# Hyena filter spectrum by folded lags: tap pairs summed and differenced over n and 512 - n, two lag tiles per frequency tile

## The chip, the cores and the metric

The kernel runs on one core of a Trainium2 chip. The metric is the device time of one execution in microseconds (us). Engines: PE (TensorE, matmuls), DVE (VectorE), ACT (ScalarE), POOL (GpSimd), SP (SyncE, which issues most of the DMAs).

## The reference

Two transformer-like blocks run one after the other on x of shape (1, 512, 1024) in float32. The first mixes a Hyena branch (512 channels) and a bidirectional mLSTM branch, then has cross attention to a memory of 256 tokens and a feed-forward layer; the second has a gated convolution, a linear recurrent unit and a gated feed-forward layer. What the change touches is the spectrum of the Hyena filters:

```python
def _hyena_filter_spectrum(L, w1, b1, fr1, w2, b2, fr2, w3):
    ...
    hid = jnp.sin(fr2.astype(f32) * (hid @ w2.astype(f32) + b2.astype(f32)))
    filt = (hid @ w3.astype(f32)).reshape(L, HYENA_ORDER, FILTER_DIRS, D_HYENA)
    ...
    filt = filt * jnp.exp(-t * jnp.abs(deltas))[:, None, None, :]
    fwd = filt[:, :, 0]
    bwd = jnp.flip(filt[1:, :, 1], axis=0)
    two_sided = jnp.concatenate([fwd, jnp.zeros((1, HYENA_ORDER, D_HYENA), f32), bwd], axis=0)
    return jnp.fft.rfft(two_sided, axis=0)
```

L is 512. The real part of the spectrum at frequency k is a cosine sum over the lags n = 0 to 511 of (forward tap + backward tap), the imaginary part a sine sum of their difference, with angle 2 pi n k / 1024; frequency 512 has the alternating sum alone.

## The kernel before

All weights come through one ring of four 128x1024 **strips**: SP loads strip n into slot n % 4 once PE has finished strip n - 4 (semaphore `pe_done`, lines 455 to 465). ACT casts the strip to its fp32r high part (`high`, line 1003), POOL writes the low part (`low`, line 479), and PE makes every product out of three fp32r matmuls: high x high, high x low, low x high (`three`, lines 518 to 520). Each engine works down a queue in program order; ACT's calls `ahead(n)` cast strip n + 3. All order is written by hand with semaphores, and nothing is scheduled by a planner.

**Start, v/o strips and units.** PE goes through eight v/o strips (`vo_strip`, lines 585 to 587), four on banks 0 to 3 and four on banks 4 to 7 of the accumulator. Among their matmuls stand eight **units** (`unit(q)`, line 564), one for each order (2) and tile of 128 lags (4). A unit is two fp32 matmuls on `hid` and `hneg` (the hidden layer with the sign of the backward half turned), which give the sum and the difference of the forward and backward taps of these 128 lags; for the tile that holds lag 0 the skip gain is added by one matmul with a single row (line 568). Unit 2 waits for ACT to have copied v out of banks 0 to 3 (`vo_kept`, tile `VX`, line 1105). DVE multiplies a unit by the decay (`sum_and_difference`, line 1492, tile `sd`), ACT casts it into the high half of its tap pair (`unit_high`, line 1063), DVE writes the low half (`unit_low`, line 1499, semaphore `f_pair`). Tap pairs are the tiles `taps`, 128 lags x (512 sum + 512 difference).

**Spectrum.** When all eight pairs are there, PE goes through five steps s, one strip each (`for s in range(N_SPEC)`). Step s, for s from 0 to 3, gives 128 frequencies: for part 0 (cosine, on the sums) and part 1 (sine, on the differences) and both orders it contracts over four lag tiles, 4 x 3 matmuls a bank, four banks. Step 4 is frequency 512 alone, two banks. Even steps use banks 0 to 3, odd ones banks 4 to 7. In the middle of step 0 stand two fp32 matmuls with `ones` (lines 627 and 628): the column sums of squares of the memory (`mem_sq`, reduced by DVE at line 1528) and of x. ACT empties the banks (`spectrum(s)`, line 1131) into `Hc`, `Hs` and `HB` and signals `spec_out`; between these stand the norm's Sqrt, the casts of the memory (`NH`) and the strips' casts.

**After it** come the gate strip, eight q/k strips with their convolution on DVE, the z strips beside the mLSTM, and the rest of both blocks.

Of the kernel before, what the change touches and what calls it, by code (L numbers as in the profile page):

```python
# [35 lines left out]
P = 128  # L36
T = 512
# [10 lines left out]
N_VO, N_SPEC, N_GATE, N_QK, N_Z, N_HY = 8, 5, 1, 8, 12, 4  # L48
# [37 lines left out]
UNITS = 2 * (T // P)  # L86
STEPS = 4 * 2 * TT
# [71 lines left out]
def build(nc, A, out):  # L159
    ctx = ExitStack()  # L160
    with ctx:
# [24 lines left out]
        sd = [at(f"sd{i}", 2 * T, (164 + 4 * i) * KB + 128) for i in range(2)]  # L186
# [75 lines left out]
        acc = at("acc", T, small + 13856)  # L262
        misc = at("misc", 80, small + 15904)
# [67 lines left out]
        f_pair = sem("f_pair")  # L331
        norm_sum = sem("norm_sum")
# [181 lines left out]
        def _(pe):  # L514
# [97 lines left out]
            for s in range(N_SPEC):  # L612
                n = S_SPEC + s
                pe.wait_ge(lo_ready, (n + 1) * 2)
# [14 lines left out]
                mm.then_inc(pe_done, 1)  # L629

            strip(S_GATE, S_GATE % RING, 2, XH, XL)
            for u in range(N_QK):
                strip(S_QK + u, (S_QK + u) % RING, (u + 3) % 4, XH, XL,
                      taken=E_GATE + u - 2 if u >= 3 else None, needs=(spec_out, N_SPEC) if u in (1, 2) else None)
# [363 lines left out]
        def _(act):  # L998
# [86 lines left out]
            act.activation(hneg[:], hid[:], ACT.Copy, scale=col("sgn")).then_inc(f_neg, 1)  # L1085
# [30 lines left out]
            ahead(7)  # L1116
            act.wait_ge(pe_done, S_VO + 8)
# [308 lines left out]
        def _(dve):  # L1426
# [58 lines left out]
            def sum_and_difference(q):  # L1485

                dve.wait_ge(f_tap, q + 1)
                if q >= 2:
                    dve.wait_ge(f_pair, q - 1)
                b = (4, 6, 0, 2, 0, 2, 0, 2)[q]  # L1490
                dec = tile(decay, q % TT).rearrange("p (a c) -> p a c", a=1).to_broadcast([P, 2, T])
                dve.tensor_tensor(sd[q % 2][:].rearrange("p (a c) -> p a c", a=2), ps[:, b:b + 2, :], dec, ALU.mult
                                  ).then_inc(f_sd, 1)
                dve.wait_ge(f_sd, q + 1)

            def unit_low(q):
# [637 lines left out]
def _tables():  # L2134
    n = np.arange(T)[:, None]
    k = np.concatenate([np.arange(0, T, 2), np.arange(1, T, 2)])[None, :]
    ang = 2 * np.pi * ((n * k) % (2 * T)) / (2 * T)
    cos, sin = np.cos(ang), np.sin(ang)
    cos_nyq = cos.copy()
    cos_nyq[:, 0] = np.where(np.arange(T) % 2 == 0, 1.0, -1.0)  # L2140
# [13 lines left out]
    spec = [[blk(cos, k_, s) for k_ in range(TT)] + [blk(sin, k_, s) for k_ in range(TT)] for s in range(TT)]  # L2154
    spec.append([blk(cos_nyq, k_, 0) for k_ in range(TT)] + [zero] * TT)
# [13 lines left out]
    return spec, order, feat, decay  # L2169
# [112 lines left out]
```

## Time and profile before

| | |
|---|---|
| median of 3 runs | 1810.19 us (1808.28 to 1810.41) |
| the profiled execution's own time | 1808.34 us |
| its span, first to last instruction | 1806.5 us |
| mean granted clock of PE | 0.983 of full |
| PE busy | 1735.1 us, 96% of the span |
| ACT, DVE, POOL busy | 667.0, 877.3, 831.5 us |
| spectrum stage | 83.2 us to 139 us of the span |

The profile is one execution. Times in the rows are microseconds from the start of the span; "busy" is the time in which an engine had an instruction running, and a window's row gives the busy time and the number of instructions of each engine in turn. A timeline's row begins with start and length in us, "x2" stands for two such instructions in a row, and the bracket at its end tells how long the engine was idle before and whose result ended that. The matmuls overlap: one of 128x512 lasts 0.39 us in a row and the next starts 0.23 us after it.

### The profile page before, as it was taken

Reading aid. Unit: us, or ns where it says so; the run is one execution under the profiler, and the core shown is the slowest. Engines: PE = TensorE matmul, PEld = TensorE weight load, DVE = VectorE, ACT = ScalarE, POOL = GpSimd, SP = SyncE. Lnnn points to the kernel's source line nnn. Section 1 sums busy time; section 2 is a strip of 40 time slices with the busy share of each in tenths; the row PEclk is TensorE's granted clock in tenths of the full one; section 3 lists DMA queues with packets and bytes.
Section 4 is the critical chain, followed back from the end, with each engine's and each line's share of the span. In section 5 each row is a group of like instructions: output and inputs, shape, how many; then the busy total and the mean of one; then the engine's idle time right before and its main releaser. Section 6 shows DMA issues by size and latency. Waiting matters only on the chain.

```text
span 1806.5 us, 21589 instructions
## 1 busy us (share of the span) xinstructions
PE 1735.1 (96%) x7584; PEld 1398.8 (77%) x7584; DVE 877.3 (49%) x1163; ACT 667.0 (37%) x850; POOL 831.5 (46%) x614
## 2 busy tenths in 40 slices
PE   7999999888998999999999999999999999999996
PEld 4677767776785888888888788888888888888885
DVE  6447666776425371424255767664333343132235
ACT  4434344434423322111124566665333432222222
POOL 4324422467540354444443666565444354444443
PEclk9999999889999999999999999999999999999998
DMA  5112211125220222222222333332222222322222
GB/s 199 59 40 89 70 48 47 70 94 175 85 92 19 97 94 93 93 95 99 97 93 93 108 102 117 105 116 93 93 102 96 94 93 95 103 93 93 104 94 93
DMA packets 47631, 168.60 MB, mean 93 GB/s; under 512 B 5141, under 2 KB 5269, under 8 KB 47322
## 3 DMA queue, kind: packets, MB, share of 16 engines
q1 hardware_dynamic: 46016, 163.75, 26.3%
q10 hardware_dynamic: 1562, 4.13, 0.6%
q8 instruction: 35, 0.57, 0.1%
q14 instruction: 18, 0.15, 0.0%
HBM read 165.76 MB, written 2.10 MB: 93 GB/s over the span
## 4 chain that ended last, share of the span: by engine, by line
PE 42%; issue 21%; POOL 14%; DVE 2%; POOLq 0%; ACT 0%; DMA 0%; DVEq 0%; SPq 0%
PE ps L518 14%; POOL m_w_lo L479 14%; PE ps L519 14%; PE ps L520 14%; DVE m_h L2129 0%; DVE m_ZL L1748 0%; DVE m_qs L1738 0%; DVE m_TM L1822 0%; DVE m_s L1440 0%; DMA m_raw<-in_strips 0%; DVE m_s L1818 0%; POOL m_QL L497 0%; POOLq L487 0%; DVE m_QL L1810 0%; POOLq L485 0%
## 5 line engine op out<-in xcount | busy, mean ns | idle before, releaser
L479 POOL TENSOR_TENSOR m_w_lo<-m_raw,m_w_hi 128x512 fp32r<-128x512 f32 x604 | 816.7, 1374 | 939.1 <-ACT m_w_hi L1003 939.0
L1003 ACT ACTIVATE m_w_hi<-m_raw 128x1024 fp32r<-128x1024 f32 x302 | 318.7, 1057 | 626.7 <-DMA m_raw<-in_strips 626.4
L518 PE MATMUL ps<-m_XH,m_w_hi 128*128 128x512 f32 x1096 | 440.2, 402 | 5.5 <-POOL m_w_lo L479 5.1
L520 PE MATMUL ps<-m_XH,m_w_lo 128*128 128x512 f32 x1096 | 429.4, 392 | 0.0
L519 PE MATMUL ps<-m_XL,m_w_hi 128*128 128x512 f32 x1000 | 392.1, 392 | 0.0
L518 PEld LDWEIGHTS ps<-m_XH,m_w_hi 128*128 128x128 f32 x1096 | 207.6, 189 | 59.5 <-issue 10.4
L520 PEld LDWEIGHTS ps<-m_XH,m_w_lo 128*128 128x128 f32 x1096 | 207.3, 189 | 43.8
L519 PEld LDWEIGHTS ps<-m_XL,m_w_hi 128*128 128x128 f32 x1000 | 189.7, 190 | 40.5 <-issue 2.0
L518 PE MATMUL ps<-m_FH,m_w_hi 128*128 128x512 f32 x432 | 168.3, 390 | 0.3 <-DVE m_FL L1433 0.3
L519 PE MATMUL ps<-m_FL,m_w_hi 128*128 128x512 f32 x432 | 168.2, 389 | 0.0
L520 PE MATMUL ps<-m_FH,m_w_lo 128*128 128x512 f32 x432 | 168.2, 389 | 0.0
L518 PE MATMUL ps<-m_YH,m_w_hi 128*128 128x512 f32 x384 | 152.5, 397 | 0.0
L520 PE MATMUL ps<-m_YH,m_w_lo 128*128 128x512 f32 x384 | 151.7, 395 | 0.0
L519 PE MATMUL ps<-m_YL,m_w_hi 128*128 128x512 f32 x384 | 151.7, 395 | 0.0
L518 PEld LDWEIGHTS ps<-m_FH,m_w_hi 128*128 128x128 f32 x432 | 81.1, 188 | 17.6 <-DVE m_FL L1433 0.7
L520 PEld LDWEIGHTS ps<-m_FH,m_w_lo 128*128 128x128 f32 x432 | 81.1, 188 | 16.8
L519 PEld LDWEIGHTS ps<-m_FL,m_w_hi 128*128 128x128 f32 x432 | 81.1, 188 | 16.8
L519 PEld LDWEIGHTS ps<-m_YL,m_w_hi 128*128 128x128 f32 x384 | 72.2, 188 | 17.7 <-issue 0.5
L518 PEld LDWEIGHTS ps<-m_YH,m_w_hi 128*128 128x128 f32 x384 | 72.2, 188 | 17.6 <-issue 0.5
L520 PEld LDWEIGHTS ps<-m_YH,m_w_lo 128*128 128x128 f32 x384 | 72.2, 188 | 17.2
L1969 DVE TENSOR_TENSOR m_h<-m_h,ps 128x512 f32 x24 | 16.5, 688 | 106.2 <-PE ps L520 106.2
L2101 DVE TENSOR_TENSOR m_s<-ps,m_rstd 128x512 f32<-128x512 f32 x22 | 15.2, 691 | 97.1 <-PE ps L520 97.1
(335 smaller groups left out, 2289.4 us busy)
## 6 DMA issues: line engine op xcount, KB each, us to landing
m_raw<-in_strips SPq DMA_DIRECT2D x302, 512.0 KB, 3.2
m_x_in<-in_x SPq DMA_DIRECT2D x4, 512.0 KB, 11.8
m_x_res<-in_x ACTq DMA_DIRECT2D x1, 2048.0 KB, 8.3
out<-m_h SPq DMA_DIRECT2D x8, 256.0 KB, 2.2
m_decay<-in_decay ACTq DMA_DIRECT2D x1, 1024.0 KB, 10.4
m_memf<-in_mem SPq DMA_DIRECT2D x1, 1024.0 KB, 16.5
m_w<-in_w ACTq DMA_DIRECT2D x1, 512.0 KB, 8.1
m_const<-in_const ACTq DMA_DIRECT2D x1, 256.0 KB, 6.9
```

The source lines that it names most:

```text
L479: nc.gpsimd.tensor_tensor(w_lo[:, c], raw[:, c], f(w_hi[:, c]), ALU.subtract).then_inc(lo_ready, 1)
L518: pe.matmul(dst, w_hi[:, c], xh, start=first, stop=False)
L519: pe.matmul(dst, w_hi[:, c], xl, start=False, stop=False)
L520: return pe.matmul(dst, w_lo[:, c], xh, start=False, stop=last)
L1003: act.activation(w_hi[:, c], raw[:, c], ACT.Copy).then_inc(hi_ready, 1)
L1969: dve.tensor_tensor(hm, hm, ps[:, u, :], ALU.add).then_inc(evac, 1)
L2101: dve.tensor_tensor(s0[:], ps[:, u, :], rstd[:], ALU.mult).then_inc(evac, 1)
```

## The change

The cosine at frequency k and lag 512 - n is the cosine at lag n times +1 for even k and -1 for odd k, the sine the other way round. So after the decay DVE adds and subtracts the tap tiles of lags n and 512 - n (`folded`), and every frequency tile contracts over 256 lags instead of 512. For that, the features and the decay are laid out so that tile 2 holds lag 256 and then 511 down to 385, tile 3 the lags 384 to 257, and the units are made in the order of tiles 0, 2, 1, 3. Frequencies are sorted into multiples of 4, those with rest 2, and the odd ones. Lag 0 and lag 256 have no partner; their share is put right by the first row of the tables, and in three of the steps by two matmuls a bank that contract over one row (`coef`, which ACT writes). One strip now serves two steps: three strips instead of five.

```diff
-N_VO, N_SPEC, N_GATE, N_QK, N_Z, N_HY = 8, 5, 1, 8, 12, 4
+N_VO, N_SPEC, N_GATE, N_QK, N_Z, N_HY = 8, 3, 1, 8, 12, 4
...
+UNIT_TILE = (0, 2, 1, 3)
...
-                o, tt = divmod(q, TT)
+                o, tt = q // TT, UNIT_TILE[q % TT]
...
-            for s in range(N_SPEC):
-                n = S_SPEC + s
-                pe.wait_ge(lo_ready, (n + 1) * 2)
+            for s in range(5):
+                n, odd = S_SPEC + s // 2, s in (2, 3)
+                if s % 2 == 0:
+                    pe.wait_ge(lo_ready, (n + 1) * 2)
...
-                for part in range(2 if s < 4 else 1):
+                for part in ((0, 1), (1, 0), (0, 1), (0, 1), (0,))[s]:
+                    edge = part == 0 and s in (1, 2, 3)
+                    if s == 1 and edge:
+                        pe.wait_ge(coef_in, 2)
                     for o in range(2):
-                        for k in range(TT):
-                            mm = three(ps[:, (s % 2) * 4 + part * 2 + o, :], n % RING, part * TT + k,
-                                       tap(part, 0, o * TT + k), tap(part, 1, o * TT + k), k == 0, k == TT - 1)
+                        dst = ps[:, (s % 2) * 4 + part * 2 + o, :]
+                        for k in range(2):
+                            u = 2 * (2 * o + k) + (odd if part == 0 else not odd)
+                            mm = three(dst, n % RING, ((s % 2) * 2 + part) * 2 + k, tap(part, 0, u), tap(part, 1, u),
+                                       k == 0, k == 1 and not edge)
+                        if edge:
+                            c, u = slice((s > 1) * P, ((s > 1) + 1) * P), 4 * o + (s == 1)
+                            for half in range(2):
+                                mm = pe.matmul(dst, coef[0:1, c], tap(0, half, u)[0:1, :], start=False, stop=half == 1)
...
-                mm.then_inc(pe_done, 1)
+                mm.then_inc(spec_mid if s in (0, 2) else pe_done, 1)
...
             def unit_high(q):
 
-                act.wait_ge(f_sd, q + 1)
-                act.activation(tap_pair(0, q), sd[q % 2][:], ACT.Copy).then_inc(f_hi, 1)
+                act.wait_ge(f_fold, q + 1)
+                act.activation(tap_pair(0, q), (evens_, odds)[q % 2][q // 2 % 2][:], ACT.Copy).then_inc(f_hi, 1)
...
+            act.wait_ge(ld_mem, 16)
+            act.activation(mem_sq[:], memf[:], ACT.Square).then_inc(mem_sqr, 1)
             act.wait_ge(pe_done, S_VO + 8)
...
-            act.wait_ge(ld_mem, 16)
-            act.activation(mem_sq[:], memf[:], ACT.Square).then_inc(mem_sqr, 1)
...
-                ahead(S_SPEC + s)
-                act.wait_ge(pe_done, S_SPEC + s + 1)
+                if s % 2 == 0:
+                    ahead(S_SPEC + s // 2)
+                if s == 0:
+                    act.wait_ge(norm_all, 2)
+                    for i in range(2):
+                        act.activation(coef[0:1, i * P:(i + 1) * P], ones[0:1, :], ACT.Copy, scale=1.0 - 0.5 * i
+                                       ).then_inc(coef_in, 1)
+                if s in (0, 2):
+                    act.wait_ge(spec_mid, s // 2 + 1)
+                else:
+                    act.wait_ge(pe_done, S_SPEC + (s + 1) // 2 + (s == 4))
...
+            def folded(pair):
+
+                dve.wait_ge(f_sd, 2 * pair + 2)
+                if pair >= 2:
+                    dve.wait_ge(f_pair, 2 * pair - 3)
+                odd = odds[pair % 2]
+                dve.tensor_tensor(evens_[pair % 2][:], sd_a[:], odd[:], ALU.add).then_inc(f_fold, 1)
+                dve.wait_ge(f_fold, 2 * pair + 1)
+                dve.tensor_tensor(odd[:], sd_a[:], odd[:], ALU.subtract).then_inc(f_fold, 1)
...
-            for q in range(UNITS):
-                sum_and_difference(q)
-                if q:
-                    unit_low(q - 1)
+            for pair in range(UNITS // 2):
+                damped(2 * pair)
+                damped(2 * pair + 1)
+                if pair:
+                    unit_low(2 * pair - 2)
+                    unit_low(2 * pair - 1)
+                folded(pair)
+            unit_low(UNITS - 2)
             unit_low(UNITS - 1)
```

`damped(q)` is the old `sum_and_difference(q)` (the product with the decay, now line 1523), which writes to `sd_a` for even q and to one of two tiles `odd` for odd q; for the first unit of a pair it waits for the previous pair's `folded`.

DVE's queue at its first taps, before. The names `m_sd` are the damped units, `m_taps` the tap pairs; `f_tap` is PE's signal that a unit is made:

```order
L1492 TENSOR_TENSOR m_sd_67<-ps,m_decay 128x1024 [waits f_tap,ld_decay]
L1492 TENSOR_TENSOR m_sd_68<-ps,m_decay 128x1024 [waits f_tap,f_sd]
L1499 TENSOR_TENSOR m_taps_60<-m_sd_67,m_taps_60 128x1024 [waits f_hi,f_sd]
L1492 TENSOR_TENSOR m_sd_67<-ps,m_decay 128x1024 [waits f_pair,f_tap]
L1499 TENSOR_TENSOR m_taps_60<-m_sd_68,m_taps_60 128x1024 [waits f_hi,f_sd]
```

The same place in the change:

```order
L1523 TENSOR_TENSOR m_sd_a<-ps,m_decay 128x1024 [waits f_tap,ld_decay]
L1523 TENSOR_TENSOR m_odd_68<-ps,m_decay 128x1024 [waits f_tap]
L1532 TENSOR_TENSOR m_even_70<-m_sd_a,m_odd_68 128x1024 [waits f_sd]
L1534 TENSOR_TENSOR m_odd_68<-m_sd_a,m_odd_68 128x1024 [waits f_fold]
L1523 TENSOR_TENSOR m_sd_a<-ps,m_decay 128x1024 [waits f_fold,f_tap]
L1523 TENSOR_TENSOR m_odd_69<-ps,m_decay 128x1024 [waits f_tap]
L1539 TENSOR_TENSOR m_taps_60<-m_even_70,m_taps_60 128x1024 [waits f_hi]
```

Sum and difference of a pair stand between the damping of its second unit and the first low part, and the low parts come two units later.

ACT's queue at the same place in the change; before, it has the same rows, but the two casts to `m_taps` read `m_sd` and wait for `f_sd`:

```order
L1081 ACTIVATE m_taps_60<-m_even_70 128x1024 [waits f_fold]
L1021 ACTIVATE m_w_hi<-m_raw 128x1024 [waits landed2]
L1081 ACTIVATE m_taps_60<-m_odd_68 128x1024 [waits f_fold]
L1123 ACTIVATE m_VX<-ps,m_misc 128x4x128 [waits c_root,pe_done]
L1123 ACTIVATE m_VX<-ps,m_misc 128x4x128 x3
L1021 ACTIVATE m_w_hi<-m_raw 128x1024 [waits landed3]
```

The copies of v (`m_VX`) stand behind both casts, so behind both results of the first `folded`.

PE's queue in step 2 of the change, the first two banks (cosine, orders 0 and 1):

```order
L525 MATMUL ps<-m_taps_60,m_w_hi 128x512 [waits spec_out,lo_ready]
L526 MATMUL ps<-m_taps_60,m_w_hi 128x512
L527 MATMUL ps<-m_taps_60,m_w_lo 128x512
L525 MATMUL ps<-m_taps_61,m_w_hi 128x512
L526 MATMUL ps<-m_taps_61,m_w_hi 128x512
L527 MATMUL ps<-m_taps_61,m_w_lo 128x512
L641 MATMUL ps<-m_taps_60,m_coef 128x512 x2
L525 MATMUL ps<-m_taps_62,m_w_hi 128x512
```

Before, a bank has twelve rows of this kind; now it has six, and two matmuls with `m_coef` in the banks of the cosine part of steps 1, 2 and 3.

## Rows read from the trace of the kernel before

**Rows 1.** The page, part 1: busy time, share of the span, instructions.
```profile
PE 1735.1 (96%) x7584; PEld 1398.8 (77%) x7584; DVE 877.3 (49%) x1163; ACT 667.0 (37%) x850; POOL 831.5 (46%) x614
```

**Rows 2.** The windows of six stretches (columns in the first row).
```profile
core 0: us, PE busy (x) PEld busy (x) DVE busy (x) ACT busy (x) POOL busy (x), PEclk, DMA share, GB/s
32.60:35.20 2.60, 0.02 (x2) 0.04 (x1) 2.41 (x2) 1.68 (x2) 2.12 (x2) 1.00 0.53 191
37.40:40.70 3.30, 3.30 (x9) 2.62 (x8) 0.00 (x0) 0.42 (x1) 2.52 (x2) 0.51 0.00 0
48.10:49.60 1.50, 0.04 (x1) 0.02 (x1) 1.32 (x2) 0.10 (x1) 1.47 (x2) 1.00 0.62 246
88.70:91.60 2.90, 0.17 (x1) 0.03 (x1) 2.76 (x1) 0.00 (x0) 2.46 (x2) 1.00 0.00 0
91.90:95.20 3.30, 3.30 (x7) 1.94 (x6) 1.27 (x3) 0.00 (x0) 0.00 (x0) 0.50 0.00 0
100.30:139.00 38.70, 38.70 (x169) 31.57 (x169) 12.38 (x44) 18.78 (x33) 9.97 (x7) 1.00 0.16 55
```

**Rows 3.** The tile `m_taps` from 83 to 140 us: duration min/median/max in ns.
```profile
L518 PE MATMUL ps<-m_taps,m_w_hi x72: 388/393/1415, 83.2 to 138.1; 128*128 128x512 f32 x72
```

**Rows 4.** The timeline of ACT, spectrum stage: start, length, line, operation.
```profile
100.33 1.09 ACT L1131 ACTIVATE m_Hc<-ps 128x512 f32<-128x512 f32 x2 [11.75 <-PE ps L520]
...
139.02 0.60 ACT L1131 ACTIVATE m_HB<-ps 128x512 f32<-128x512 f32 x1 [1.15 <-PE ps L520]
```

**Rows 5.** The timeline of DVE, 48 to 92 us.
```profile
48.24 1.23 DVE L1492 TENSOR_TENSOR m_sd<-ps,m_decay 128x1024 f32<-128x1024 f32 x1 [3.28 <-PE ps L564]
...
77.93 1.23 DVE L1492 TENSOR_TENSOR m_sd<-ps,m_decay 128x1024 f32<-128x1024 f32 x1 [2.00 <-PE ps L564]
...
79.19 2.36 DVE L1499 TENSOR_TENSOR m_taps<-m_sd,m_taps 128x1024 fp32r<-128x1024 f32 x2
...
87.68 3.78 DVE L1528 TENSOR_REDUCE m_s<-m_mem_sq 128x256 f32<-128x2048 f32 x1 [6.12 <-ACT m_mem_sq L1122]
```

**Rows 6.** The timeline of ACT, 45 to 88 us.
```profile
45.96 1.04 ACT L1003 ACTIVATE m_w_hi<-m_raw 128x1024 fp32r<-128x1024 f32 x1
...
49.50 1.07 ACT L1063 ACTIVATE m_taps<-m_sd 128x1024 fp32r<-128x1024 f32 x1 [2.50 <-DVE m_sd L1492]
...
50.47 2.41 ACT L1105 ACTIVATE m_VX<-ps,m_misc 128x512 f32<-128x512 f32 x4
...
85.71 1.93 ACT L1122 ACTIVATE m_mem_sq<-m_memf 128x2048 f32<-128x2048 f32 x1
```

**Rows 7.** The timeline of PE, 53 to 92 us.
```profile
53.79 1.02 PE L564 MATMUL ps<-m_w,m_hid 128*128 128x512 f32 x2
...
61.34 1.02 PE L564 MATMUL ps<-m_w,m_hid 128*128 128x512 f32 x2
...
64.54 0.39 PE L586 MATMUL ps<-m_w_hi,m_XL 128*128 128x512 f32 x1
...
67.04 1.02 PE L564 MATMUL ps<-m_w,m_hid 128*128 128x512 f32 x2
...
67.90 1.02 PE L564 MATMUL ps<-m_w,m_hneg 128*128 128x512 f32 x2
...
68.99 0.40 PE L586 MATMUL ps<-m_w_hi,m_XL 128*128 128x512 f32 x1
...
91.61 0.97 PE L627 MATMUL ps<-m_s,m_const 128*128 128x256 f32 x2 [2.74 <-DVE m_s L1528]
```

**Rows 8.** The timelines of DVE and POOL, 72 to 166 us.
```profile
157.56 2.13 DVE L1630 TENSOR_TENSOR m_gA<-m_gA,m_gF 4x1024 f32<-4x1024 f32 x1
...
163.78 1.21 DVE L1638 TENSOR_TENSOR m_gE<-m_gE,m_gF 4x1024 f32<-4x1024 f32 x1
...
72.31 2.53 POOL L479 TENSOR_TENSOR m_w_lo<-m_raw,m_w_hi 128x512 fp32r<-128x512 f32 x2 [7.67 <-ACT m_w_hi L1003]
...
156.89 3.96 POOL L479 TENSOR_TENSOR m_w_lo<-m_raw,m_w_hi 128x512 fp32r<-128x512 f32 x2 [10.75 <-ACT m_w_hi L1003]
```

More of the change, by code:

```diff
@@ L185, in build @@
         decay = at("decay", TT * T, 156 * KB + 128)
-        sd = [at(f"sd{i}", 2 * T, (164 + 4 * i) * KB + 128) for i in range(2)]
+        sd_a = at("sd_a", 2 * T, 164 * KB + 128)
+        odds = [at("odd0", 2 * T, 168 * KB + 128), at("odd1", 2 * T, 176 * KB + 128)]
+        evens_ = [at("even0", 2 * T, 180 * KB + 128), at("even1", 2 * T, 184 * KB + 128)]
         hid = at("hid", T, 172 * KB + 128)
@@ L262, in build @@
         acc = at("acc", T, small + 13856)
+        coef = at("coef", 2 * P, small + 13856, F32R)
         misc = at("misc", 80, small + 15904)
@@ L331, in build @@
         f_pair = sem("f_pair")
+        f_fold = sem("f_fold")
+        coef_in = sem("coef_in")
+        spec_mid = sem("spec_mid")
         norm_sum = sem("norm_sum")
@@ L633, in _ @@
                 strip(S_QK + u, (S_QK + u) % RING, (u + 3) % 4, XH, XL,
-                      taken=E_GATE + u - 2 if u >= 3 else None, needs=(spec_out, N_SPEC) if u in (1, 2) else None)
+                      taken=E_GATE + u - 2 if u >= 3 else None, needs=(spec_out, 5) if u in (1, 2) else None)
             def transposed(bank, b):
@@ L1084, in _ @@
             act.wait_ge(f_sin, 3)
-            act.activation(hneg[:], hid[:], ACT.Copy, scale=col("sgn")).then_inc(f_neg, 1)
+            act.activation(hneg[:, 1:T], hid[:, 1:T], ACT.Copy, scale=col("sgn")).then_inc(f_neg, 1)
             ahead(1)
@@ L1483, in x_low, with damped @@
                                          ALU.mult, ALU.subtract).then_inc(x_ready, 1)
-            def sum_and_difference(q):
+            def damped(q):
+                pair = q // 2
                 dve.wait_ge(f_tap, q + 1)
-                if q >= 2:
-                    dve.wait_ge(f_pair, q - 1)
+                if q % 2 == 0 and pair:
+                    dve.wait_ge(f_fold, 2 * pair)
+                if q % 2 and pair >= 2:
+                    dve.wait_ge(f_pair, 2 * pair - 2)
                 b = (4, 6, 0, 2, 0, 2, 0, 2)[q]
-                dec = tile(decay, q % TT).rearrange("p (a c) -> p a c", a=1).to_broadcast([P, 2, T])
-                dve.tensor_tensor(sd[q % 2][:].rearrange("p (a c) -> p a c", a=2), ps[:, b:b + 2, :], dec, ALU.mult
+                dst = odds[pair % 2] if q % 2 else sd_a
+                dec = tile(decay, UNIT_TILE[q % TT]).rearrange("p (a c) -> p a c", a=1).to_broadcast([P, 2, T])
+                dve.tensor_tensor(dst[:].rearrange("p (a c) -> p a c", a=2), ps[:, b:b + 2, :], dec, ALU.mult
                                   ).then_inc(f_sd, 1)
-                dve.wait_ge(f_sd, q + 1)
+            def folded(pair):
[6 more added lines that the diff above has]
+                dve.tensor_tensor(odd[:], sd_a[:], odd[:], ALU.subtract).then_inc(f_fold, 1)
             def unit_low(q):
                 dve.wait_ge(f_hi, q + 1)
-                dve.tensor_tensor(tap_pair(1, q), sd[q % 2][:], f(tap_pair(0, q)), ALU.subtract).then_inc(f_pair, 1)
+                dve.tensor_tensor(tap_pair(1, q), (evens_, odds)[q % 2][q // 2 % 2][:], f(tap_pair(0, q)), ALU.subtract
+                                  ).then_inc(f_pair, 1)
             dve.memset(hid[64:P, 0:1], 0.0).then_inc(f_zero, 1)
+            dve.memset(hneg[:, 0:1], 0.0).then_inc(f_zero, 1)
             ch.add(dve.memset(VX[:].rearrange("p (a c) -> p a c", c=P + 1)[:, :, P:P + 1], 1.0))
@@ L2153, in _tables @@
     zero = np.zeros((P, P))
-    spec = [[blk(cos, k_, s) for k_ in range(TT)] + [blk(sin, k_, s) for k_ in range(TT)] for s in range(TT)]
-    spec.append([blk(cos_nyq, k_, 0) for k_ in range(TT)] + [zero] * TT)
+    spec = [[blk(part, k_, s) for s in pair for part in (cos, sin) for k_ in range(2)] for pair in ((0, 1), (2, 3))]
+    spec.append([blk(cos_nyq, k_, 0) for k_ in range(2)] + [zero] * 6)
     order = [[blk(part, t_, j) for j in pair for part in (z_cos, z_sin) for t_ in range(2)] for pair in ((0, 1), (2, 3))]
@@ L2168, in _tables @@
     decay = np.exp(-(t * np.abs(deltas)[None, :]).astype(np.float64)).astype(np.float32)
-    return spec, order, feat, decay
+    times = np.concatenate([np.arange(HALF + 1), np.arange(T - 1, HALF, -1)])
+    return spec, order, feat[times], decay[times]
 def kernel(**inputs):
```

9 lines of the change are left out of this document (6 added, 3 removed).

## The prediction

> **What bounds the kernel now.** I start from the page: TensorE (PE) is busy for 1735.1 of 1806.5 us [rows 1], so time comes out only where PE has fewer matmuls or waits less. Next the windows of the stages, to see what holds PE in the one that is changed. In the spectrum stage, 100.3 to 139.0 us, PE is busy the whole 38.70 us at full clock [rows 2], while DVE works 12.4, ACT 18.8 and POOL 10.0 us beside it. Its matmuls are 216 (three lines of 72, the first at 83.2 us, the last at 138.1 us) [rows 3]. ACT's evictions mark the ends of the steps: Hc of step 0 starts at 100.33, HB of step 4 at 139.02 [rows 4], so steps 1 to 3 (48 matmuls each) and step 4 (24) took 38.69 us for 168 matmuls, 0.230 us each. This stage is PE's, and a matmul less is 0.230 us less. Ahead of it the picture is another one: PE ran through from the last v/o strip into step 0 at 83.2 us, because the last of the eight tap pairs was ready at 79.19 + 2.36 = 81.55 us [rows 3, 5], with 1.7 us to spare; and within step 0 it stood from 88.7 to 91.6 us [rows 2] for the memory norm (DVE's reduction, 87.68 + 3.78 us) [rows 5]. So a longer DVE or ACT chain in front of step 0 is paid for at once.
>
> **Removed matmuls.** Each output bank contracts over two tiles of 128 lags instead of four. Steps 0 to 3 have 24 instead of 48, step 4 has 12 instead of 24: 108 fewer. 96 of these lie behind the memory norm (12 in the second half of step 0, 72 in steps 1 to 3, 12 in step 4): 96 x 0.230 = 22.1 us. The 12 ahead of the norm are worth nothing, since PE waits there anyway. Two strips less are loaded and split; PE waits for none of them in this stage, so this I cost at nothing: it is hidden under PE's matmuls, which need one strip per two steps now, some 14 us, against 1.04 us of ACT for its cast and 2.53 us of POOL for its split [rows 6, 8].
>
> **Added matmuls.** Six banks get an edge term of two matmuls that contract over one row. The trace has such a one in the skip term, in fp32. A unit with it takes 61.34 to 64.54 = 3.20 us up to the second matmul of the strip behind it, one without it 67.04 to 68.99 = 1.95 us [rows 7]. So it adds 1.25 us, where a full-height fp32 matmul takes 67.04 to 67.90 = 0.86 us: 0.39 us goes to changing from 128 rows to one and back. I take two matmuls at the stage's pace plus one such change, 0.46 + 0.39 = 0.85 us a bank, 5.1 us in all. From below it is 12 x 0.230 = 2.8 us (no price for the change), from above the whole 1.25 us a bank, 7.5 us.
> The Trainium skill says, in TensorEngine Tiling, Key Properties, that a change of the tiling mode drains the engine; the 0.39 us agree. The Trainium skill's TensorE: Matmul & The Clock Gate, in its closing table, has a small contraction take the same time as a full one; by that the edges would be the 2.8 us of the lower bound, and no run here yet shows which holds for this format.
>
> **The first wait, for VX.** Unit 2's matmuls wait for ACT to copy v (VX, 4 instructions) out of banks 0 to 3. Today ACT casts unit 0's pair at 45.00, a strip at 45.96 and unit 1's pair at 49.50, then copies VX from 50.47 to 52.88 us, and unit 2 starts at 53.79 without a wait [rows 6, 7]. In the change the cast of unit 0 waits for the sum of units 0 and 1, which exists only when unit 1 is damped: 48.24 + 1.23 = 49.47, sum done at 50.7, difference at 52.0 us. ACT's queue is in order, so behind it come: cast 50.8 to 51.8, the strip's cast to 52.8, the second cast to 53.8, VX to 56.2 us. PE reaches unit 2 at 53.8 and stands 2.4 us. Everything behind on PE moves by that.
> What follows such a wait is in the windows: after 2.6 us idle (32.6 to 35.2) the granted clock was 0.51 from 37.4 to 40.7, after 2.9 us (88.7 to 91.6) 0.50 from 91.9 to 95.2 [rows 2]: 1.2 GHz, and 3.4 us at half pace cost 1.7 us. After 1.5 us (48.1 to 49.6) the 18 matmuls up to 53.79 kept 0.23 us each [rows 2, 7]. 2.4 us is nearer to the first two: I add 1.7 us.
>
> **The second wait, ahead of step 0.** I count from the tap of unit 7 (77.93 us today, where DVE's damping starts) [rows 5]. Today one damping and two low parts follow (3.6 us). In the change: damping, low 4, low 5, sum, difference, low 6, low 7, seven instructions of 1.26 us, 8.8 us. PE arrives 5.3 us after the tap (83.2) and stands about 3.5 us. That alone would be free up to the norm, but the norm's chain hangs on the same difference: it is done 6.3 us after the tap, then ACT's last cast (1.06), the strip's cast (1.05), the square of mem (1.93, moved ahead of the sigmoids), DVE's reduction (3.78) [rows 5, 6], with hand-offs 14.3 us, against 91.61 - 77.93 = 13.7 today [rows 5, 7]. The sigmoids, which now stand behind the square and a table load, end at about the same moment. So the norm's matmuls start 0.6 us later, relative to the tap.
> To this comes POOL. It splits strip 9, 2.53 us long [rows 8], from about 0.5 us before the tap to 2.1 us after it, when low 4 would start at 1.3 us. DVE's additions of two SBUF operands suffer there: 4x1024 took 2.13 us with POOL at work (156.89 to 160.85) and 1.21 us without [rows 8], 0.9 us more. Bounds: 0, as for dampings (one operand in PSUM, 1.23 us beside POOL), and 1.4 us, one whole POOL instruction. I take 0.9. Norm later by 1.5 us in all.
> The Trainium skill states this as a lock: SBUF — State Buffer, "two separate sides", gives the shared port pair to GpSimd or to a two-SBUF-input DVE instruction for its whole length. It speaks against this change, which puts eight more such instructions on DVE.
>
> **Inside the steps** ACT evicts four banks in 2.2 us [rows 4] and a step is 24 x 0.230 + 1.7 = 7.2 us, so no step waits for its banks; the norm's Sqrt and the casts between fit as well. The late DVE chain (the softplus) ends about when step 4 ends, and the gate's results come 5.5 us after that: covered. From the gate strip on all is as before, shifted.
>
> **Sum**, against the profiled execution (1808.34 us, span 1806.5): +2.4 (VX) +1.7 (clock) +1.5 (norm) -22.1 (96 matmuls) +5.1 (edges) = -11.4, which gives 1797 us. The step 4 that ended at 138.9 ends near 127.5. The median of the three runs is 1.9 us above the profiled one; I keep the profiled one, the median may lie as much above. 0.2% (3.6 us) is what a measurement of this kernel can tell from no change.
>
> **Rivals.**
> 1. *A kinder clock.* PE has to stand before and inside step 0 anyway. If the clock is low only there, or does not fall after 2.4 us, one or two stretches of 1.7 us go: 1793.6 to 1795.3. For it: today's stretch of 3.3 us from 91.9 sits in the norm, where it costs, and the step 0 of 12 matmuls now lies between two waits, where it would cost nothing. Against: three waits now instead of one.
> 2. *The edges at matmul price*: 2.8 us instead of 5.1, 1794.6. For: these are fp32r with two in a row; against: the 0.39 us above.
> 3. *More on the path*: edges at 7.5 us, a further low stretch, or POOL meeting one more DVE instruction, 1.7 to 2.4 us each: 1799 to 1802.
> 4. *No gain to speak of*: PE hands over the stage and ACT's queue becomes the bound (evictions, casts, Sqrt in order). It would have to make each of steps 1 to 3 wait over 2.6 us; ACT has near 5 us to spare in each. 1805 to 1811.
> 5. *Slower*: the low clock does not end. One-row matmuls come every 3 us from step 1 on, and behind the long waits PE could be granted 1.2 GHz through the whole stage. Steps 0 to 4 hold 108 matmuls and the edges, 30 us; at half pace 26 us more with the 1.7 counted already, 1823 us. It decides once the clock is low for 23 us beyond what I counted. Against: behind the skip's one-row matmul of 62.3 us a whole unit kept its pace [rows 7], and the low stretches shown lasted 3.3 us.
>
> **How the numbers follow.** Forecast 0.46; rival 1 0.24, rival 2 0.12, rival 3 0.12, rival 4 0.03, rival 5 0.03. The unknown costs (edges 2.8 to 7.5, POOL 0 to 1.4, clock 0 to 3.4 either way) span 1790 to 1803 together; that holds all of the first four cases but extreme sums. Faster by over 0.2%: 0.94; within: 0.03; slower: 0.03.
>
> **What would show it.** Right: 108 matmuls on taps and 12 on coef; unit 2 waiting 2.4 us for VX; the first spectrum matmul 3 to 4.5 us behind the last strip's; steps 1 to 3 near 7.2 us apart; step 4 done near 127.5 us; PE's wait for a split strip among the q/k strips unchanged, only earlier. Wrong: a wait for spec_out inside the steps, edges over 1.3 us a bank, or a low clock beyond the norm.

## The result, and the profile after

| | before | after |
|---|---|---|
| median | 1810.3 us, 4 runs (1808.28 to 1814.12) | 1793.05 us, 4 runs (1790.76 to 1795.69) |
| the profiled execution's own time | 1808.34 us | 1793.52 us |
| its span | 1806.5 us | 1791.7 us |
| mean granted clock of PE | 0.983 | 0.982 |

The ratio is 0.9903, with a 95% interval of 0.9881 to 0.9924: 17 us less by the medians, five times the 3.6 us that a measurement can tell, and 14.8 us less from one profiled execution to the other. The forecast was 11.4 us less, and 1797 us, with a range of 1790 to 1803.

To see where the 14.8 us came from, I cut the stretch up to the gate strip at four moments which each have one row in either trace. **Tap**: DVE starts to damp the last unit. **Norm**: PE starts the first matmul with `ones`. **Step 0**: ACT starts to evict it. **Gate**: PE starts the gate strip.

| us | tap | norm | step 0 | gate |
|---|---|---|---|---|
| before | 77.93 | 91.61 | 100.33 | 138.82 |
| after | 81.77 | 95.78 | 100.13 | 124.46 |
| change of the stretch that ends there | +3.84 | +0.33 | -4.37 | -14.16 |

That is -14.36 us at the gate, and the remaining 0.46 us came off behind it. The medians are 2.5 us further apart than these two executions (17.25 against 14.8 us), and no trace places that part.

The page of the kernel after, part 1, against [rows 1]:

```profile
PE 1716.9 (96%) x7488; PEld 1379.8 (77%) x7488; DVE 884.3 (49%) x1172; ACT 665.2 (37%) x850; POOL 824.4 (46%) x610
```

There are 96 matmuls fewer, 108 taken away and 12 added. PE's busy time fell by 18.2 us and the span by 14.8: the rest went to PE's new waits.

The tile `m_taps` on PE, after, against [rows 3]: duration min/median/max in ns, first and last start:

```profile
L525 PE MATMUL ps<-m_taps,m_w_hi x36: 387/395/799, 90.3 to 123.8; 128*128 128x512 f32 x36
L526 PE MATMUL ps<-m_taps,m_w_hi x36: 387/393/628, 90.7 to 124.0; 128*128 128x512 f32 x36
L527 PE MATMUL ps<-m_taps,m_w_lo x36: 387/394/628, 91.0 to 124.2; 128*128 128x512 f32 x36
L641 PE MATMUL ps<-m_taps,m_coef x12: 387/444/497, 104.2 to 118.5; 1*128 1x512 f32 x12
```

The windows of the kernel after, against [rows 2] (columns in the first row):

```profile
core 0: us, PE busy (x) PEld busy (x) DVE busy (x) ACT busy (x) POOL busy (x), PEclk, DMA share, GB/s
53.70:55.90 2.20, 0.06 (x2) 0.06 (x1) 0.00 (x0) 2.20 (x5) 1.43 (x2) 1.00 0.00 0
56.80:60.10 3.30, 3.30 (x7) 1.87 (x6) 1.23 (x1) 0.00 (x0) 2.50 (x2) 0.50 0.00 0
87.10:90.30 3.20, 0.11 (x1) 0.00 (x0) 3.19 (x3) 3.00 (x4) 0.24 (x1) 1.00 0.49 164
90.50:93.90 3.40, 3.40 (x9) 2.64 (x10) 2.09 (x1) 3.37 (x4) 2.18 (x2) 0.55 0.00 0
95.80:100.10 4.30, 4.30 (x17) 3.24 (x18) 3.15 (x4) 1.17 (x3) 2.52 (x2) 1.00 0.00 0
100.10:124.40 24.30, 24.30 (x96) 16.87 (x96) 13.21 (x45) 15.86 (x30) 2.54 (x2) 1.00 0.12 42
```

PE stands in the first and the third of these. Behind each comes a stretch with a granted clock near 0.5, 1.2 GHz. The last row is the spectrum stage from the eviction of step 0 on: PE is busy for all of its 24.30 us at full clock, as it was for 38.70 us before.

The timeline of PE, after (start, length, line, operation; the bracket is the idle time before it and who ended it), against [rows 7]:

```profile
55.84 1.26 PE L572 MATMUL ps<-m_w,m_hid 128*128 128x512 f32 x2 [2.14 <-ACT m_VX L1123]
...
90.34 0.50 PE L525 MATMUL ps<-m_taps,m_w_hi 128*128 128x512 f32 x1 [3.13 <-DVE m_taps L1539]
...
95.78 0.67 PE L645 MATMUL ps<-m_s,m_const 128*128 128x256 f32 x2 [0.82 <-DVE m_s L1574]
...
103.85 0.39 PE L527 MATMUL ps<-m_taps,m_w_lo 128*128 128x512 f32 x1
104.17 0.73 PE L641 MATMUL ps<-m_taps,m_coef 1*128 1x512 f32 x2
104.83 0.50 PE L525 MATMUL ps<-m_taps,m_w_hi 128*128 128x512 f32 x1
105.17 0.39 PE L526 MATMUL ps<-m_taps,m_w_hi 128*128 128x512 f32 x1
```

These are the three waits of the prediction: 2.14 us for `VX`, 3.13 us ahead of step 0 for the last low part, 0.82 us ahead of the norm. The last four rows are an edge, the two one-row matmuls between the last matmul of one bank and the first of the next. From line 527 to the line 526 behind it there are 1.32 us, and without an edge there would be two starts, 0.46 us: an edge is 0.86 us.

PE's weight loads (PEld) at the same place show where the time over two matmuls goes:

```profile
103.62 0.19 PEld L527 LDWEIGHTS ps<-m_taps,m_w_lo 128*128 128x128 f32 x1
104.17 0.29 PEld L641 LDWEIGHTS ps<-m_taps,m_coef 1*128 1x128 f32 x2 [0.36 <-issue]
104.83 0.19 PEld L525 LDWEIGHTS ps<-m_taps,m_w_hi 128*128 128x128 f32 x1 [0.37 <-issue]
```

The load for the matmul of 103.85 started 0.23 us ahead of it. The load for the first one-row matmul started only with it, at 104.17, and so did the load for the first full one behind, at 104.83. The second one-row matmul starts at 104.51. So the four steps from 103.85 to 105.17 take 0.32, 0.34, 0.32 and 0.34 us instead of 0.23: 0.20 us more on the way to one row, and 0.20 us more on the way back.

The timeline of ACT, after, against [rows 4, 6]:

```profile
50.53 1.06 ACT L1081 ACTIVATE m_taps<-m_even 128x1024 fp32r<-128x1024 f32 x1 [12.82 <-DVE m_even L1532]
...
53.39 2.40 ACT L1123 ACTIVATE m_VX<-ps,m_misc 128x512 f32<-128x512 f32 x4
...
100.13 1.09 ACT L1158 ACTIVATE m_Hc<-ps 128x512 f32<-128x512 f32 x2 [2.27 <-PE ps L527]
...
107.19 1.09 ACT L1158 ACTIVATE m_Hc<-ps 128x512 f32<-128x512 f32 x2 [1.10 <-PE ps L641]
...
114.65 1.09 ACT L1158 ACTIVATE m_Hc<-ps 128x512 f32<-128x512 f32 x2 [3.12 <-PE ps L527]
...
121.90 1.09 ACT L1158 ACTIVATE m_Hc<-ps 128x512 f32<-128x512 f32 x2 [3.66 <-PE ps L527]
```

`VX` is copied at 53.39, 2.9 us later than before. Steps 2 and 3 end 7.25 us apart, where 7.2 was written down; at every one of them ACT had been idle before (1.10, 3.12, 3.66 us), so it never held the stage.

The timelines of DVE and POOL, after, against [rows 5, 8]:

```profile
81.77 1.23 DVE L1523 TENSOR_TENSOR m_odd<-ps,m_decay 128x1024 f32<-128x1024 f32 x1 [1.76 <-PE ps L572]
82.91 1.50 DVE L1539 TENSOR_TENSOR m_taps<-m_even,m_taps 128x1024 fp32r<-128x1024 f32 x1
84.33 1.21 DVE L1539 TENSOR_TENSOR m_taps<-m_odd,m_taps 128x1024 fp32r<-128x1024 f32 x1
85.47 1.21 DVE L1532 TENSOR_TENSOR m_even<-m_sd_a,m_odd 128x1024 f32<-128x1024 f32 x1
86.72 1.23 DVE L1534 TENSOR_TENSOR m_odd<-m_sd_a,m_odd 128x1024 f32<-128x1024 f32 x1
...
91.81 3.82 DVE L1574 TENSOR_REDUCE m_s<-m_mem_sq 128x256 f32<-128x2048 f32 x1 [1.52 <-ACT m_mem_sq L1136]
...
80.80 2.52 POOL L486 TENSOR_TENSOR m_w_lo<-m_raw,m_w_hi 128x512 fp32r<-128x512 f32 x2 [7.67 <-ACT m_w_hi L1021]
```

POOL's split runs to 83.32. The damping beside it, with one operand in PSUM, keeps its 1.23 us; the low part that starts at 82.91 takes 1.50 instead of 1.21 us.

### The profile page after: what moved, and what is told of

Its sections match the earlier page's. It is cut to its first block, busy times and chain, and to the rows that moved or that the text cites. A ratio compares the mean times of both kernels' runs of the same rounds, so it can differ in the third digit from the quotient of the medians.

```text
span 1791.7 us, 21383 instructions
## 1 busy us (share of the span) xinstructions
PE 1716.9 (96%) x7488; PEld 1379.8 (77%) x7488; DVE 884.3 (49%) x1172; ACT 665.2 (37%) x850; POOL 824.4 (46%) x610
## 4 chain that ended last, share of the span: by engine, by line
PE 43%; issue 21%; POOL 14%; DVE 2%; POOLq 0%; ACT 0%; DMA 0%; DVEq 0%; SPq 0%
POOL m_w_lo L486 14%; PE ps L525 14%; PE ps L526 14%; PE ps L527 14%; DVE m_TM L1868 0%; DVE m_h L2175 0%; DVE m_qs L1784 0%; DVE m_s L1467 0%; DVE m_ZL L1794 0%; DMA m_raw<-in_strips 0%; DVE m_s L1864 0%; POOL m_QL L504 0%; POOLq L494 0%; DVE m_QL L1856 0%; POOLq L492 0%
## 6 DMA issues: line engine op xcount, KB each, us to landing
m_decay<-in_decay ACTq DMA_DIRECT2D x1, 1024.0 KB, 10.2
```

## The experiments

Theory A was the prediction's reading: every term of its sum is a wait or a length that can be taken away by itself, with the sizes above. The rival B differed from run to run, as the quoted texts say. All ratios are to the kernel before, timed beside the run. Its median there was 1804.5 to 1808.0 us and not 1810.3, so the absolute times that the quoted texts forecast, which start from the first comparison, are some 2 to 6 us too high, and it is the ratios and the rows that can be compared.

**VX copied before the first casts.** ACT's two casts of the first pair go behind the four copies.

```diff
             ahead(2)
-            unit_high(0)
             ahead(3)
-            unit_high(1)
...
                                ).then_inc(vo_kept, 1)
+            unit_high(0)
+            unit_high(1)
             ahead(4)
```

> The change, but ACT copies v (VX) out of its banks before it casts the first two tap pairs. Theory A (the wait of 2.1 us for VX and the low clock of 3.4 us behind it lie on the path): unit 2 starts without a wait, no low clock near 57 us, the tap of the last unit is 3.8 us earlier (78.0 instead of 81.8), step 4 ends 3.8 us earlier (120.6 instead of 124.4), the time is 1789.2 against 1793.0. Theory B (DVE's chain of sums and differences is the true limit ahead of step 0, and the wait for VX only runs beside it): the wait goes, but the one ahead of step 0 grows by as much, and the time stays at 1793.

Measured: 1787.31 us, ratio 0.9893 (0.9874 to 0.9912). The tap stands at 77.31 instead of 81.77, the norm at 91.29, step 0 at 97.14, the gate at 121.48. Windows and PE's row of this run:

```profile
90.50:94.50 4.00, 3.21 (x6) 1.94 (x7) 1.34 (x3) 1.78 (x4) 2.42 (x2) 0.57 0.00 0
...
91.29 1.19 PE L645 MATMUL ps<-m_s,m_const 128*128 128x256 f32 x2 [2.38 <-DVE m_s L1574]
```

The wait for `VX` and the low clock behind it were worth 4.5 us at the tap, 0.4 of which is this profile's own front; the table above has 3.84. But only 3.0 us of it are left at the gate, because the low clock now fell from 90.5 on, onto the norm: from norm to step 0 it took 5.85 us instead of 4.35. In the times even less can be seen: against the ratios of the kernel after (0.9903, and 0.9906 below) this is about 2 us less, where A had 3.8, and the intervals overlap. So A holds for the wait by the rows, and a low stretch is not simply removed with its wait: it can turn up at the next one.

**No edges.** The 12 one-row matmuls are left out, and with them the correction for lags 0 and 256 in steps 1 to 3.

```diff
-                    edge = part == 0 and s in (1, 2, 3)
+                    edge = False
```

> The change without the twelve one-row matmuls of the edges (the share of lags 0 and 256 in three steps is left out). Theory A (0.85 us a bank: two matmuls and a change of the rows there and back): steps 1, 2 and 3 are 1.7 us shorter each, 5.1 us together, the time is 1787.9. Theory B (a one-row matmul costs what a full one does): 0.46 us a bank, 2.8 us together, 1790.2.

Measured: 1784.21 us, ratio 0.9882 (0.9862 to 0.9902). The timeline of ACT of this run, steps 2 and 3:

```profile
109.04 1.09 ACT L1158 ACTIVATE m_Hc<-ps 128x512 f32<-128x512 f32 x2 [0.93 <-PE ps L527]
...
114.56 1.09 ACT L1158 ACTIVATE m_Hc<-ps 128x512 f32<-128x512 f32 x2 [1.94 <-PE ps L527]
```

A step takes 5.52 us here and 7.25 with two edges, 0.87 us an edge. Norm to gate is 23.48 us instead of 28.68: 5.20 us for six edges. The 5.1 us of the sum are shown, and the rival that had them at the price of two matmuls (2.8 us) is out.

This run shows one thing more, ahead of anything that it changes. Its tap stands at 79.62, 2.15 us earlier than in the kernel after, though PE waited for `VX` as long as there (2.11 us). Its own front is 0.55 us of that. The rest is the clock behind that wait. The windows of this run, the wait and what followed:

```profile
53.20:55.30 2.10, 0.04 (x1) 0.00 (x0) 0.00 (x0) 2.10 (x5) 1.43 (x2) 1.00 0.00 0
56.20:59.60 3.40, 3.40 (x12) 2.08 (x11) 1.22 (x1) 0.04 (x1) 2.52 (x2) 1.00 0.00 0
```

No low clock followed here. Of the six profiles with a wait of 2.10 to 2.14 us for `VX`, three have a low stretch of 3.4 us behind it (the kernel after, the run without the first half of step 0, the run with the memory early) and three have none (this one, the run with every matmul twice, the kernel after once more).

**First half of step 0 left out.** The cosine part of step 0 isn't computed.

```diff
-                        for k in range(2):
+                        for k in range(2) if (s, part) != (0, 0) else ():
```

> The change without the twelve matmuls of the first half of step 0 (the cosine part of the first frequency tile is left out). Theory A (these run while PE would wait anyway, and cost nothing): the norm's matmuls start at 95.8 us as before this edit, and what follows is unchanged. Theory B (they take the low clock that the wait ahead of them brings, so that it is over when the norm comes): without them the wait lasts from 87 to 95.8 us, the low clock falls on the norm and the second half, and step 4 ends 1.7 us later, 126.1 instead of 124.4.

Measured: one run, 1795.82 us. PE's row and the windows of this run:

```profile
94.33 1.19 PE L645 MATMUL ps<-m_s,m_const 128*128 128x256 f32 x2 [8.55 <-ACT m_TM L1139]
...
89.00:94.30 5.30, 0.00 (x0) 0.00 (x0) 3.69 (x1) 5.27 (x7) 2.21 (x2) 0.51 0.00 0
94.30:99.50 5.20, 5.17 (x10) 3.50 (x11) 2.62 (x3) 1.23 (x3) 2.49 (x2) 0.51 0.00 0
```

The norm came 13.99 us behind the tap, with the 12 matmuls 14.01: they cover the wait and cost nothing, as costed. But with the one wait of 8.55 us came a low clock of 10.2 us, and norm to step 0 took 6.77 instead of 4.35 us. Here the work in front of the wait is worth nothing as work and 2.4 us as what keeps the low clock off the path behind it. That was B's side of this run, which had 1.7 us for it. It is one profile; in the second one of the kernel after, norm to step 0 took 4.69 us.

**Every spectrum matmul twice.** Each bank adds its two lag tiles twice (the result is doubled, apart from the edges).

```diff
-                        for k in range(2):
+                        for kk in range(4):
+                            k = kk % 2
...
-                                       k == 0, k == 1 and not edge)
+                                       kk == 0, kk == 3 and not edge)
```

> The change with every bank of the spectrum contracted twice over its two lag tiles (the output is twice the spectrum in all but the edges), so that PE has as many matmuls as in the kernel before, and sums, differences and edges besides. Theory A (a matmul is worth 0.23 us behind the norm): 96 matmuls behind the norm give 22.1 us, the twelve ahead of it overhang the norm by 1.8 us, 1817 us in all, 6.5 us above the kernel before, which is what the front and the edges cost. Theory B (the stage was held by ACT's evictions or by strips and not by matmuls): less than 15 us above the change, under 1808.

Measured: 1816.87 us, ratio 1.0057 (1.0038 to 1.0076). PE's rows of this run, norm and gate:

```profile
98.58 0.59 PE L646 MATMUL ps<-m_s,m_const 128*128 128x256 f32 x2
...
149.21 0.39 PE L525 MATMUL ps<-m_XH,m_w_hi 128*128 128x512 f32 x1
```

Norm to gate is 50.63 us against 28.68: 21.95 us for 96 matmuls, 0.229 each, the largest term of the sum. It is also the answer to what the change costs without its gain: with before's number of matmuls it is slower than before by 10.4 us at the gate, 5.1 at the tap, 1.85 in the norm and 3.4 behind it (5.1 of edges, less the low clock that left the norm). By the ratio it is 0.4 to 0.8% slower, 7 to 14 us, where 6.5 us was written. The 1817 us of the text was hit only because the kernel before ran at 1804.5 us beside it. The 5.1 us at the tap are the wait for `VX`, 2.1, a front that was 1.2 us later, and a low stretch of 6.8 instead of 3.4 us in that front, 1.7.

**Square and reduction of the memory moved to the start.** Both go ahead of the decay, so that the norm no longer hangs on the DVE chain behind the last tap.

```diff
             ahead(0)
+            act.wait_ge(ld_mem, 16)
+            act.activation(mem_sq[:], memf[:], ACT.Square).then_inc(mem_sqr, 1)
             act.wait_ge(f_arg, 2)
...
+            dve.wait_ge(mem_sqr, 1)
+            dve.tensor_reduce(s0[:, 0:MEM], ...).then_inc(mem_sum, 1)
             dve.wait_ge(ld_decay, 16)
```

> The change with the square of mem and DVE's reduction of it moved to the start, into 2 us and 4 us in which ACT and DVE idle. Theory A (the norm is then held by PE itself, whose first half of step 0 ends only 5.1 us after its start, because it runs at the low clock): the norm's matmuls start 0.8 us earlier relative to the last tap, 13.2 us behind it instead of 14.0, and nothing else moves. Theory B (the chain square, reduction is what the norm waits for, and without it the sigmoids alone): 12.1 us behind the tap, 1.9 us gained.

Measured: one run, 1793.9 us. PE's rows of this run:

```profile
90.36 0.79 PE L525 MATMUL ps<-m_taps,m_w_hi 128*128 128x512 f32 x1 [3.14 <-DVE m_taps L1539]
...
94.73 0.59 PE L645 MATMUL ps<-m_s,m_const 128*128 128x256 f32 x2
```

The wait ahead of the norm is gone, and the norm comes 12.95 us behind the tap (A 13.2, B 12.1): the wait ahead of step 0 and the half step behind it at low clock set it now. In this profile the two waits stand behind one another, and taking the second away gives 1.1 us. The time of a single run says nothing about 1.1 us.

**All of it together.** `VX` first, memory early, the sigmoids and their table load ahead of the last strip's cast, step 0 bank by bank in the order of the pairs, and the norm behind step 0 instead of inside it. The cut shows PE's new order of step 0 only.

```diff
-            pe.wait_ge(f_pair, UNITS)
             for s in range(5):
...
+                if s == 0:
+                    banks = [(0, 0), (1, 0), (0, 1), (1, 1)]
...
+                    if s == 0:
+                        pe.wait_ge(f_pair, (4, 4, 7, 8)[at_])
```

> The change with its waits taken away: ACT copies VX before the first casts; the square and reduction of mem at the start; the sigmoids ahead of the cast of strip 10, with their table load moved into an idle stretch of ACT; step 0 takes both banks of order 0 first, so that it waits for tap pairs 6 and 7 only halfway, and the norm's two matmuls come behind step 0. Theory A (the waits ahead of step 0 and of the norm were the whole cost of the front): PE waits under 0.5 us between the last v/o strip and the gate strip, no low clock there, the gate strip starts 35.7 us behind the tap of the last unit instead of 42.7 and 4 us more is gained ahead of that tap; some 10.8 us under the change, a ratio to the kernel before of 0.984. Theory B (DVE's and ACT's longer chain comes back behind the norm, as a wait for rstd, spec_out or the gate's results): under 6 us gained.

Measured: 1782.71 us, ratio 0.9855 (0.9832 to 0.9877). The windows of this run:

```profile
35.00:41.80 6.80, 6.27 (x19) 5.33 (x20) 4.51 (x4) 2.10 (x3) 4.27 (x4) 0.51 0.14 52
79.50:92.30 12.80, 12.80 (x56) 10.21 (x55) 9.38 (x9) 7.33 (x13) 3.75 (x4) 1.00 0.21 76
92.30:116.20 23.90, 23.90 (x95) 16.52 (x94) 15.20 (x47) 15.30 (x31) 5.45 (x5) 1.00 0.12 41
```

From the tap to the gate it is 36.59 us (35.7 was written), 42.69 in the kernel after, and PE has no wait and no low clock in it. The tap came only 2.2 us earlier, where 4 us was written. The whole came to 6.4 us (next run) and not to A's 10.8, just above B's 6. The first row shows where a low clock still was: behind the wait of 2.57 us for the column sums of x, at 33 us, for 6.8 us.

**The kernel after once more, and the one with all of it once more.** There is no new edit; the kernel after ran on the same chip as the run just told, the other one on the chip of the last run below.

> The change once more, on the chip and in the rounds of the runs beside it, as their yardstick. Both theories: the ratio to the kernel before as in the first comparison, 0.990, and the same order of events ahead of the gate strip.

> The kernel with all the waits of the front taken away once more, as the yardstick of the run beside it. Both theories: a ratio to the kernel before of 0.9855.

Measured: the kernel after 1789.07 us, 0.9906 (0.9888 to 0.9924); the other 1782.03 us, 0.9862 (0.9835 to 0.9889). Side by side on one chip, the orders of the run above are worth 1789.07 - 1782.71 = 6.4 us, and from tap to gate 6.4 in the profiles (43.03 against 36.59). The kernel after had its gate at 125.06 and yet a span of 1784.5 us, 7.2 less than in its first profile. The windows of the first 400 us, the first profile of the kernel after and then this one:

```profile
0.00:400.00 400.00, 354.53 (x1548) 269.66 (x1548) 280.86 (x424) 173.04 (x272) 153.13 (x108) 0.93 0.22 79
0.00:400.00 400.00, 352.18 (x1576) 269.12 (x1577) 282.54 (x428) 176.38 (x276) 163.06 (x112) 0.97 0.25 85
```

A mean clock of 0.93 is near 55 us at half pace, one of 0.97 near 27 us, and this profile has one more low stretch of 3.4 us behind it, at 526. So it had about 24 us less at half pace, worth up to 12 us of time, which is enough for the 7.2 us of the spans. (Both profiles end with 11 to 15 us of low clock in which PE has next to nothing left to do.)

**Useless matmuls in the waits.** On top of the `VX` edit, 13 matmuls ahead of step 0 and 10 ahead of the norm, on a bank that is overwritten.

```diff
+            pe.wait_ge(lo_ready, (S_SPEC + 1) * 2)
+            pe.wait_ge(f_sd, UNITS)
+            for _ in range(13):
+                pe.matmul(ps[:, 0, :], w_hi[:, 0:P], XH[:, 0:T], start=True, stop=True)
             pe.wait_ge(f_pair, UNITS)
...
                     if s == 0 and part == 0:
+                        for _ in range(10):
+                            pe.matmul(ps[:, 2, :], w_hi[:, 0:P], XH[:, 0:T], start=True, stop=True)
```

> The kernel with VX copied first, and 13 matmuls without use (fp32r, 128x512) in PE's wait ahead of step 0 and 10 in the wait ahead of the norm; they write to free banks. Theory A (the low clock comes from PE's idle stretches): the clock stays full from 60 us to the q/k strips, the norm starts as before 14.0 us behind the last tap, and from the norm to the end of step 0 it takes 4.4 us instead of 5.9; 1.5 us less than with VX copied first alone. Theory B (the low clock comes from something else, such as the one-row or fp32 matmuls): it stays, and the fillers cost up to 1 us.

Measured: 1786.19 us, ratio 0.9889 (0.9867 to 0.9911). The windows of this run:

```profile
77.60:91.70 14.10, 13.75 (x59) 10.62 (x57) 12.46 (x8) 8.93 (x10) 4.21 (x4) 1.00 0.18 67
91.80:96.10 4.30, 4.30 (x17) 3.24 (x18) 3.16 (x4) 1.01 (x4) 2.53 (x2) 1.00 0.00 0
```

Without the waits there is no low clock: 1.00 in both stretches, and norm to step 0 is 4.34 us again, where the same kernel without the fillers took 5.85. This run ties the low clock of this place to the waits, since nothing else of the work differs. It is one profile, but the others bear it out: all eight with waits of 2.7 us or more between the tap and the end of step 0 (the kernel before among them) have a low stretch there, and the four in which PE doesn't wait there (this one, all of it together, twice, and the last run) have none. The gate stands 1.05 us ahead of that kernel's. In the times it can't be seen: 0.9889 against 0.9893.

**The column sums of x as well.** The kernel with all of it, and PE's column sums (four matmuls, eight rows in the trace) stand behind the second token tile of the fourth v/o strip instead of ahead of it, where their data is there.

```diff
+                    if n == 3 and tt == 1:
+                        pe.wait_ge(ld_blocks, 16)
+                        pe.wait_ge(norm_sum, 1)
+                        for t_ in range(TT):
+                            cm = pe.matmul(ps[:, 6, t_:t_ + 1], ...)
+                        cm.then_inc(x_cols, 1)
                     if tt in units:
```

> The same, and the four small matmuls for the column sums of x (until now ahead of v/o strip 3, where PE waits 2.5 us for DVE's sum) put behind the second of its four token tiles. Theory A (a wait of more than 2 us in front costs itself and a low clock of 3.4 or 6.8 us behind it): no wait there, no low clock between 30 and 60 us, the last unit's tap 4.2 to 5.9 us earlier, a ratio near 0.983. Theory B (the front is held by DVE's chain of dampings, sums and differences, once PE comes earlier): PE waits for f_sd or tap pairs instead, and under 2 us is gained.

Measured: 1777.05 us, ratio 0.9838 (0.9814 to 0.9863), the lowest of all. That is 5.0 us under the kernel with all of it beside it (0.9862), and the intervals of the two overlap. The windows of this run:

```profile
39.50:43.50 4.00, 4.00 (x9) 2.45 (x9) 3.40 (x2) 0.71 (x1) 4.00 (x4) 0.57 0.00 0
76.60:113.20 36.60, 36.60 (x148) 26.64 (x147) 24.58 (x55) 22.55 (x42) 9.13 (x8) 1.00 0.16 52
```

The wait at 33 us is gone, and the tap came 2.6 to 3.0 us earlier where 4.2 to 5.9 was written. Part of the miss is this profile's own start, 1.3 us later; the other part is the clock: a low stretch of 3.4 us came at 40 all the same, and PE's timeline shows no wait between 14 and 40 us. What stands in its place is the group of column sums, eight rows of 128x1 at 36.7, 0.95 us; whether they have to do with it wasn't tried. From tap to gate it is 36.60 us, as in the run before.

## Why the prediction was right

The time lay in the range, and most of the signs that were named came: 108 matmuls on taps and 12 on `coef`, a wait of 2.14 us for `VX`, the first spectrum matmul 3.5 us behind the last strip's, steps 2 and 3 7.25 us apart, the wait for a split strip among the q/k strips unchanged at 3.7 us and 14.4 us earlier. But 1793.05 us is not the forecast's 1797. It is the time that rival 1, the kinder clock, had been given (1793.6 to 1795.3), and the gate came at 124.5 where 127.5 was written. The terms one by one:

1. **96 matmuls, -22.1 us.** Right: 21.95 us when they are put back.
2. **Edges, +5.1 us.** Right: 5.2 us when they are left out. The number came from the skip's one-row matmul [rows 7], another format and one matmul instead of two; the excursion to one row cost the same 0.4 us there and here. The Trainium skill's TensorE: Matmul & The Clock Gate, closing table, has a small contraction take the time of a full one, which gives 2.8 us as an estimate; the runs decide for 0.86 us an edge.
3. **VX and the low clock behind it, +2.4 and +1.7 us.** Right as a sum, 3.84 us. The wait was 2.14 us and the low stretch behind it the other 1.7. The first is sure: it came in all six profiles. The second was luck in part, since it came in three of the six. ACT's operations start 0.95 us apart though each lasts 1.05, so the chain of three ahead of `VX` is shorter than the sum of the lengths.
4. **Norm, +1.5 us.** Too large: +0.33. POOL was costed at 0.9 us, as if a DVE addition beside it were slow for its whole length like the 4x1024 one [rows 8]. It also had the split end 2.1 us behind the tap, and it ended 1.55 us behind it. So the low part started 0.4 us before POOL's split ended, and lost 0.28 us. The Trainium skill's SBUF — State Buffer, "two separate sides", describes a lock for the length of an instruction. These rows agree roughly: a DVE addition that comes late in POOL's instruction loses no more than what is left of it. It is one case: no other DVE addition starts beside a POOL split between 48 and 92 us. The longer chain was costed at 0.6 us and took 0.05: on DVE too an instruction that needs nothing of the one before starts 1.14 us after one of 1.21 to 1.23, where 1.26 was counted.
5. **Step 0, nothing beyond the 12 matmuls.** This is the term that failed: norm to step 0 fell by 4.37 us, of which 12 matmuls are 2.76. The sum kept the low stretch of the kernel before in the norm and added one more. The other 1.6 us is rival 1, the low stretch that lay in the norm before (91.9 to 95.2 [rows 2]) and lies ahead of it now, at 90.5 to 93.9, where PE would have waited anyway.
6. **Stage behind it.** From step 0 to the gate -14.16 us, where terms 1 and 2 leave -14.24.

Terms 3, 4 and 5 missed by 0.3, 1.2 and 1.6 us, all to the same side, and 0.46 us came off behind the gate; that is the 3.4 us by which the gain was put too low for these two executions. By the medians it was put 5.9 us too low, and the 2.5 us between the two stay open. Rival 4 is out, since ACT was idle before each eviction that ends a step, and rival 5 too, with a clock of 1.00 from 95.8 to 124.4. What isn't settled is the low clock as such: fillers take it away ahead of step 0 and the norm, but the same wait of 2.1 us for `VX` had it behind it only every other time, and in the last run a stretch of it came without a wait to point at.

## What to carry to other kernels

When a change takes work from the bounding engine, cost the chain in front of the new work with the same care: here the gain of 22 us shrank to 17 by the edges and by another 4 at an ACT queue in which two early casts stood ahead of copies that PE needed. Moving the two casts behind the copies takes that wait away, and 3.0 us of it reached the gate strip. Price a matmul with few rows by its change of shape too, not by its columns alone. Whether several of them can share one change wasn't run. Ask of every wait not only how long it is but what stands behind it: the half pace that follows costs nothing if it falls on work that waits anyway.

## What was not expected of the hardware

- **The same wait is followed by a low clock in one execution and not in the next.** Near 0.5 (1.2 GHz), for 3.4 or 6.8 us, it came behind ten of eleven waits of 1.96 to 2.60 us for the column sums, but behind only three of six of 2.10 to 2.14 us for `VX`. It came behind none of the twelve waits of 1.41 to 1.48 us that end at 48 to 52 us. And it came without any wait, at 40 us in the last run.
- **The share of low clock differs between executions of the same kernel**: about 55 and 31 us ahead of the last microseconds in the two profiles of the kernel after, with spans 7.2 us apart. A single profile of the span isn't a measure of a gain of this size. The four moments above are a better one, since they lie inside one stage, but they carry the clock of their own stretch too: the tap of the unchanged front moved by 2.15 us between two profiles.
- **An instruction's length is not its pace.** ACT's 1.05 us casts follow one another in 0.95 us, DVE's instructions of 1.21 to 1.23 us in 1.14 us when they don't depend on each other. A chain of such instructions that is costed by lengths comes out 8 to 10% too long; the difference that waits for the sum before it starts 1.25 us behind it.
- **One-row matmuls cost two changes of shape**: a pair of them takes 0.86 us in a stream whose matmuls take 0.23 us each, 0.20 us more on the way in and 0.20 us on the way out, and at both the weight load starts with its matmul instead of 0.23 us ahead.
